# Two attention stages that share buffers, later group ends, and softmax maxima and inverse sums carried to their rows by DMA through DRAM instead of by TensorE transposes

## The reference

```python
def _causal_softmax_attention(q, k, v):
    ...
        z = jnp.einsum('bhqd,bhkd->bhqk', qi, k).astype(jnp.float32) * scale
        causal = key_pos[None, :] <= q_pos[:, None]
        p = jax.nn.softmax(jnp.where(causal, z, neg), axis=-1)
        return jnp.einsum('bhqk,bhkd->bhqd', p.astype(v.dtype), v)
...
    o_mla = o_mla.transpose(0, 2, 1, 3).reshape(B, S, MLA_WIDTH) * jax.nn.silu(g_mla)
    mixed = jnp.concatenate([o_sb, o_mla], axis=-1)
    return x + gate * (mixed @ w_out)
```

## Time and profile before

| | us |
|---|---|
| median of 3 runs | 2162.2 |
| lowest and highest | 2160.57, 2168.74 |
| profiled execution | 2165.11 |
| its span, first to last instruction | 2163.4 |
| TensorE matmuls busy | 1924.4 (89%) |
| VectorE busy | 1239.1 (57%) |
| GpSimd busy | 1011.9 (47%) |
| ScalarE busy | 953.3 (44%) |

### The profile page before, as it was taken

One profiled execution on the slowest core, in us unless ns is written; L12 is line 12 of the kernel. 1 busy time (PEld: TensorE's weight loads), 2 busy tenths in 40 slices (PEclk: granted clock), 3 DMA queues, 4 the chain that ended last, 5 costly groups with the idle time before them and its releaser, 6 DMA issues. The chain is left out here.

```text
span 2163.4 us, 32782 instructions
## 1 busy us (share of the span) xinstructions
PE 1924.4 (89%) x9697; PEld 1571.3 (73%) x9697; DVE 1239.1 (57%) x1862; ACT 953.3 (44%) x1894; POOL 1011.9 (47%) x1035
## 2 busy tenths in 40 slices
PE   6389999997999997598989889499999999985998
PEld 1258888886999996377777777278787887874886
DVE  1731111114555555598989888378787888872111
ACT  1521111114333333377767667367676775762000
POOL 0400000000333333199889889567777776781122
PEclk9689999998999998699999999789899998997999
DMA  8326563445455554732517150453342534105664
GB/s 293 106 78 185 155 180 107 136 151 186 163 195 185 187 179 136 180 72 62 142 36 180 32 125 0 110 115 79 78 107 51 117 78 86 52 20 194 194 183 147
DMA packets 225371, 273.69 MB, mean 127 GB/s; under 512 B 13776, under 2 KB 161520, under 8 KB 219616
## 3 DMA queue, kind: packets, MB, share of 16 engines
q1 hardware_dynamic: 219936, 259.76, 42.4%
q10 hardware_dynamic: 5312, 12.58, 1.8%
HBM read 159.06 MB, written 109.05 MB: 124 GB/s over the span
## 5 line engine op out<-in xcount | busy, mean ns | idle before, releaser
L1944 POOL TENSOR_TENSOR mla_wl<-mla_w,mla_wh 128x512 fp32r<-128x512 f32 (+1 forms) x320 | 374.6, 1184 | 158.5 <-ACT mla_wh L1980 150.6
L1465 POOL TENSOR_TENSOR sb_wl<-sb_wf,sb_wh 128x512 fp32r<-128x512 f32 (+2 forms) x240 | 285.5, 1190 | 19.2
L1563 DVE TENSOR_TENSOR_SCAN sb_w<-sb_kp,sb_w,sb_beside 128x512 f32<-128x512 f32 x192 | 245.4, 1278 | 36.9 <-ACT sb_kp L1486 20.6
L1979 ACT ACTIVATE mla_w<-mla_zt 128x512 f32<-128x512 f32 (+1 forms) x320 | 170.6, 533 | 126.8 <-PE mla_zt L2133 62.9
L568 PE MATMUL pt_po<-h_hi,pt_wh 128*128 128x512 f32 x512 | 200.3, 391 | 9.4 <-DVE pt_wl L499 9.4
L569 PE MATMUL pt_po<-h_lo,pt_wh 128*128 128x512 f32 x512 | 199.9, 390 | 0.0
L570 PE MATMUL pt_po<-h_hi,pt_wl 128*128 128x512 f32 x512 | 199.9, 390 | 0.0
L2021 DVE TENSOR_REDUCE mla_nmx<-mla_zn 128x1 f32<-128x512 f32 (+2 forms) x320 | 191.8, 601 | 11.2 <-PE mla_zn L2100 7.3
L1486 ACT ACTIVATE sb_kp<-sb_z 128x512 f32<-128x512 f32 (+3 forms) x320 | 168.4, 530 | 33.7 <-PE sb_z L1646 16.1
L1643 PE MATMUL sb_z<-sb_kk,sb_qh 128*128 128x512 f32 (+3 forms) x320 | 132.8, 415 | 54.8 <-ACT sb_kp L1486 30.3
L1463 POOL CAST sb_wh<-sb_wf 128x512 fp32r<-128x512 f32 (+2 forms) x240 | 142.1, 592 | 72.3 <-ACT sb_wf L1497 61.8
(11 more groups left out here) (229 smaller groups left out, 4384.5 us busy)
## 6 DMA issues: line engine op xcount, KB each, us to landing
mod_wada<-in_w_ada SPq DMA_DIRECT2D x6, 2048.0 KB, 8.4
qk_mla<-tk_th SPq DMA_DIRECT2D x64, 192.0 KB, 2.1
qk_mla<-tk_tl SPq DMA_DIRECT2D x64, 192.0 KB, 2.3
mod_x<-in_x ACTq DMA_DIRECT2D x16, 512.0 KB, 4.2
pt_w<-in_w_feat SPq DMA_DIRECT2D x16, 512.0 KB, 6.0
hT<-h_hi SPq DMA_DIRECT2D x16, 512.0 KB, 3.6
hT<-h_lo SPq DMA_DIRECT2D x16, 512.0 KB, 5.2
qk_sb<-pt_oh SPq DMA_DIRECT2D x32, 256.0 KB, 2.5
```

The source lines that it names most:

```text
L1465: nc.gpsimd.tensor_tensor(wl[i][:, lo:GW], wf[i][:, lo:GW], wh[i][:, lo:GW].bitcast(F32), ALU.subtract).then_inc(s_plo, 1)
L1563: nc.vector.tensor_tensor_scan(kept, keeps, beside[:, 0:b - a], 1.0 if u["n"] == 0 else w[u["g"]][:, u["r"], b:b + 1], ALU.mult, ALU.bypas ...
L1944: nc.gpsimd.tensor_tensor(wl[i][:, cols], w[i][:, cols], wh[i][:, cols].bitcast(F32), ALU.subtract).then_inc(s_lo, 1)
L1979: nc.scalar.activation(w[i][:, cols], zt[x % 2][:, cols], ACT.Exp).then_inc(s_w, 1)
```

## The change

Three things are changed together.

Buffers: `attend_sb` and `attend_mla` use the same SBUF tensors for k, q and v (`shared`). In the last pair of the first stage SP loads q, k and v of the first softmax head into buffers that are free by then; only `kl` is left for the start of `attend_mla`. The output weights are loaded during the last pair of `attend_mla`, behind the gate. The stick-breaking stage starts when k and the last 512 queries of its first head have landed (`s_first`), part of them issued from ScalarE's queue.

Group ends: in `attend_sb`, `high` and `low` come two turns later. In `attend_mla` the quotient comes at `LAG` + 5 instead of + 2, `high` at + 7 instead of + 2, `low` and the store at + 8 instead of + 3.

Rows: `to_row` and `spread` leave TensorE, `row` and `totals` leave ScalarE. SP stores `nm` as 512 separate elements to `maxima` in DRAM, waits until they have landed, and loads them as one row into `qh`. In the same way it stores `inv` to `inverses`, waits, and loads them spread over 64 partitions into `scale`. SP now goes through the turns as the other engines do, with these steps in the order of `run`. `nm` and `inv` have two buffers each.

```diff
-        buf = {x: [m.sb(f"{x}{i}", [P, S], F32R) for i in range(2)] for x in ("kk", "qh", "ql")}
-        v = [m.sb(f"v{i}", [P, NB, P], F32R) for i in range(2)]
+        buf = {"kk": shared.kh, "qh": shared.qh, "ql": shared.ql}
+        v = shared.v
...
-            for hp in range(2):
-                load_qk(0, hp)
+            late = slice((GROUPS - 1) * GW, S)
+            for at in range(2):
+                sp.dma_start(buf["kk"][0][at * HD:(at + 1) * HD, :].bitcast(F32), qk[at, H * HD:H * HD + HD, :]
+                             ).then_inc(s_first, 16)
+            for dst, l in (("qh", 0), ("ql", 1)):
+                for at in range(2):
+                    sp.dma_start(buf[dst][0][at * HD:(at + 1) * HD, 0:late.start].bitcast(F32), qk[l, 0:HD, 0:late.start]
+                                 ).then_inc(s_qk[0], 16)
+
+            sp.sem_inc(s_qk[0], 32)
             load_v(0, 0)
+            load_qk(0, 1)
...
+                sp.wait_ge(s_z, it * U + U // 2)
+                sp.sem_inc(s_step, 1)
                 if not last:
-                    sp.wait_ge(s_z, it * U + U // 2)
-                    sp.sem_inc(s_step, 1)
                     load_qk(it + 1, 0)
-                    sp.wait_ge(s_pv, it * T + T // 2)
-                    sp.sem_inc(s_step, 1)
+                else:
+
+                    for dst, which, l, sem in ((shared.qh, 0, 0, shared.s_qkh), (shared.kh, 1, 0, shared.s_qkh),
+                                               (shared.ql, 0, 1, shared.s_qkl)):
+                        sp.dma_start(dst[0][0:QK, :].rearrange("p (n c) -> p n c", n=NB).bitcast(F32),
+                                     qkM[which, l, :, :, 0:P].rearrange("n p c -> p n c")).then_inc(sem, 16)
+                sp.wait_ge(s_pv, it * T + T // 2)
+                sp.sem_inc(s_step, 1)
+                if not last:
                     load_v(it + 1, 0)
+                else:
+                    sp.dma_start(v[0][:].bitcast(F32), vM[:, :, 0:P].rearrange("n p c -> p n c")).then_inc(shared.s_v, 16)
...
+            late = slice((GROUPS - 1) * GW, S)
+            for dst, l in (("qh", 0), ("ql", 1)):
+                for at in range(2):
+                    act.dma_start(buf[dst][0][at * HD:(at + 1) * HD, late].bitcast(F32), qk[l, 0:HD, late]
+                                  ).then_inc(s_first, 16)
...
-                for body, after in ((half_sum, AFTER), (high, AFTER + 1)):
+                for body, after in ((half_sum, AFTER), (high, AFTER + 3)):
...
-                for body, after in ((finish, AFTER), (low, AFTER + 2)):
+                for body, after in ((finish, AFTER), (low, AFTER + 4)):
...
-                if n in (0, U // 2):
+                if n == 0 and isinstance(it, int):
+
+                    pe.wait_ge(s_first, 96)
+                elif n in (0, plan.groups[0]["units"] if isinstance(it, int) else 0, U // 2):
                     pe.wait_ge(s_qk[hp], it * 96 + 96)
...
-    delays = dict(nm=-AHEAD, pm=2 - AHEAD, row=2 - AHEAD, sum=LAG, inv=LAG, spread=LAG + 1, half=LAG, sums=LAG + 1, add=LAG,
-                  gate=LAG, quotient=LAG + 2, mh=LAG + 2, ml=LAG + 3)
-    TAIL = LAG + 3
+    delays = dict(nm=-AHEAD, row=-AHEAD, sum=LAG, inv=LAG, spread=LAG, half=LAG, add=LAG,
+                  gate=LAG, quotient=LAG + 5, mh=LAG + 7, ml=LAG + 8, store=LAG + 8)
+    TAIL = LAG + 8
...
-        ps = m.ps("ps", [P, GW])
+        ps = m.ps("ps", [P, QG])
...
+            def to_row(it, hp, n):
+
+                g, head = plan.groups[n]["g"], it * 2 + hp
+                sp.wait_ge(s_nm, groups(n, it, hp) + 1)
                 sp.sem_inc(s_step, 1)
-                load_qk(it, 1)
-                reached(sp, s_pv, turns(0, it, 0))
+                sp.dma_start(maxima[bass.ds(head, 1), n, :].rearrange("o (r p) -> p (o r)", p=P),
+                             nm[n % 2][:].bitcast(F32), allow_slow_non_contiguous=True).then_inc(s_max_out, 16)
+                sp.wait_ge(s_max_out, 16 * groups(n, it, hp) + 16)
                 sp.sem_inc(s_step, 1)
-                load_v(it, 1)
-                if not start:
-                    store(it - 1, G - 1)
-
-                sp.dma_start(gate[:], gates[bass.ds(it, 1), :, :].rearrange("o p n -> p (o n)")).then_inc(s_gate, 16)
-                if not last:
-                    sp.wait_ge(s_zt, turns(0, it, 1))
+                sp.dma_start(qh[hp][QK:KP, g * GW:(g + 1) * GW].bitcast(F32), maxima[bass.ds(head, 1), n, :]
+                             ).then_inc(s_row[n % 2], 16)
+
+            def spread(it, hp, n):
+
+                g, hb, head = plan.groups[n]["g"], hp * HD, it * 2 + hp
+                sp.wait_ge(s_inv, groups(n, it, hp) + 1)
+                sp.sem_inc(s_step, 1)
+                sp.dma_start(inverses[bass.ds(head, 1), n, :].rearrange("o (r p) -> p (o r)", p=P), inv[n % 2][:],
+                             allow_slow_non_contiguous=True).then_inc(s_inv_out, 16)
+                sp.wait_ge(s_inv_out, 16 * groups(n, it, hp) + 16)
+                sp.sem_inc(s_step, 1)
+
+                reached(sp, s_scale, 16 * groups(n, it, hp))
+                sp.sem_inc(s_step, 1)
+
+                reached(sp, s_quot, pair_groups(n, it - 1) + 1)
+                sp.sem_inc(s_step, 1)
+                sp.dma_start(scale[hb:hb + HD, g * GW:(g + 1) * GW],
+                             inverses[bass.ds(head, 1), n, :].broadcast_to([HD, GW])).then_inc(s_scale, 16)
+
+            def loads(it, hp, x):
+                last = isinstance(it, int) and it == PAIRS - 1
+                if x == 0 and not (last and hp == 1):
+                    reached(sp, s_zt, turns(0, it, hp))
                     sp.sem_inc(s_step, 1)
-                    load_qk(it + 1, 0)
-                    sp.wait_ge(s_pv, turns(0, it, 1))
+                    load_qk(it + hp, 1 - hp)
+                if x == LAG + 1 and not (last and hp == 1):
+                    reached(sp, s_pv, turns(0, it, hp))
                     sp.sem_inc(s_step, 1)
-                    load_v(it + 1, 0)
-                for n in range(G - 1):
-                    store(it, n)
-
-            body(0, True, False)
-            with sp.Fori(1, PAIRS - 1) as it:
-                body(it, False, False)
-            body(PAIRS - 1, False, True)
-            store(PAIRS - 1, G - 1)
+                    load_v(it + hp, 1 - hp)
+                if x == TAIL + 1 and hp == 0:
+                    reached(sp, s_gated, pair_groups(0, it))
+                    sp.sem_inc(s_step, 1)
+                    sp.dma_start(gate[:], gates[bass.ds(it, 1), :, :].rearrange("o p n -> p (o n)")).then_inc(s_gate, 16)
+                    if last:
+                        for k in range(KD):
+                            sp.dma_start(wout.w[k][:], t["w_out"][0, k * P:(k + 1) * P, :]).then_inc(wout.s_w, 16)
+
+            sp.dma_start(kl[0][0:QK, :].rearrange("p (n c) -> p n c", n=NB).bitcast(F32),
+                         qkS[1, 1, :, :, 0:P].rearrange("n p c -> p n c")).then_inc(s_qkl[0], 16)
+            run(sp, dict(row=to_row, turn=loads, spread=spread, store=store))
...
-            def row(it, hp, n):
-
-                g = plan.groups[n]["g"]
-                act.wait_ge(s_pm, groups(n, it, hp) + 1)
-                nc.scalar.activation(qh[hp][QK:KP, g * GW:(g + 1) * GW], ps[0:1, :], ACT.Copy).then_inc(s_row, 1)
...
-            def totals(it, hp, n):
-
-                hb, g = hp * HD, plan.groups[n]["g"]
-                act.wait_ge(s_spread, groups(n, it, hp) + 1)
-
-                reached(act, s_quot, pair_groups(n, it - 1) + 1)
-                nc.scalar.activation(scale[hb:hb + HD, g * GW:(g + 1) * GW], ps[hb:hb + HD, :],
-                                     ACT.Copy).then_inc(s_scale, 1)
...
-            run(act, dict(row=row, turn=weights, half=v_low, sums=totals, mh=high))
+            run(act, dict(turn=weights, half=v_low, mh=high))
...
-                reached(dve, s_pm, groups(n, it, hp) - 1)
+                reached(dve, s_max_out, 16 * (groups(n, it, hp) - 1))
...
-                reached(dve, s_spread, groups(n, it, hp))
-                nc.vector.reciprocal(inv[:], ps[:, 0:QG]).then_inc(s_inv, 1)
+                reached(dve, s_inv_out, 16 * (groups(n, it, hp) - 1))
+                nc.vector.reciprocal(inv[n % 2][:], ps[:]).then_inc(s_inv, 1)
...
-                dve.wait_ge(s_scale, groups(n, it, hp) + 1)
+                dve.wait_ge(s_scale, 16 * groups(n, it, hp) + 16)
...
-            def to_row(it, hp, n):
-                pe.wait_ge(s_nm, groups(n, it, hp) + 1)
-
-                reached(pe, s_row, groups(n, it, hp))
-
-                reached(pe, s_scale, groups(n, it, hp) - (1 if n == 1 else 2))
-                for r in range(QG):
-                    tp = nc.tensor.transpose(ps[0:1, r * P:(r + 1) * P], nm[n % 2][:, r:r + 1], ident[:])
-                tp.then_inc(s_pm, 1)
...
                 if tn["first"]:
-                    pe.wait_ge(s_row, groups(tn["n"], it, hp) + 1)
```

(31 more changed lines are left out.)

58 lines of the change are left out of this document (33 added, 25 removed).

## The result

The changed kernel takes 2422.2 us in the median of four runs (2417.3 to 2431.8), against 2161.4 for the kernel before: ratio 1.121, interval 1.116 to 1.125. It is 12% slower, far outside the range of the prediction. The profiled execution took 2431.8 us, with a span of 2430.0.

The account below looks back on a forecast made before the run. It took TensorE to bound the second attention stage, stopped by waits for VectorE in `high`. From 2165.1 us, -109 taken away and +101 of waits behind SP's queue gave 2157, put at 2155 us, range 2105 to 2208.

Parts of the forecast that it names:

- the small transfer: Store of `nm` or sums, 512 elements of 4 bytes, to DRAM: taken to land in 3.2 us.
- the upper bound of 6.4 us: Most the element-wise store should take, from the position load of 2048 elements behind 1 MB.
- six changes and the first rows: Added waits in softmax attention: 40 us after even heads, 48 after odd ones, 6 for seven first rows.
- Rival (2): Element-wise store costs 6.4 us, not 3.2: +62 us, 2216; chance 0.32 together with another slower case.
- The loads ahead: Small transfers behind four 768 KB loads at a head's start wait for them; the loads take 18.4 us.
- A: Softmax attention: 64 sets of four transposes leave TensorE, 0.43 us a set, -28 us.
- B: Softmax attention: `high` and `low` come later after the quotient, so waits at odd heads shrink; -43 us, bounds 30 and 57.
- C: Stick-breaking stage: the same later group ends remove waits in `high`; -24 us, bounds 12 and 30.
- E: Start of softmax attention: q, k and v already loaded, but zero rows and first maxima remain; -1 us.
- D: Start of stick-breaking stage: it waits for 1.5 MB instead of 3 MB; -7 us.
- F: End of softmax attention: a round trip through DRAM replaces transposes and a copy; +4 us.
- G: Output stage: with weights loaded early it starts sooner and runs without stops; -10 us, bounds 7 and 12.

Follow-up runs that it names:

- probe: The kernel before plus a last stage where SP alone issues small transfers and waits; 512 neighbouring single elements 9.3 us, 128 of them 8.3.
- probe2: The kernel before plus a last stage of lone stores to DRAM at several spacings; 128 neighbouring elements 8.3 us, 512 elements 64 bytes apart 2.3.
- k5_loads: The changed kernel with the loads of q, k and v issued from ScalarE's queue instead of SP's; 2399.9 us, 1.110.
- k4_direct: k1_merge with the maxima written straight from SBUF into their row of SBUF by four transfers of 128 elements, without DRAM; 2093.4 us, 0.968.
- k1_merge: The changed kernel with maxima and inverse sums back on TensorE transposes; merged buffers, later group ends and early output weights stay; 2099.8 us, 0.970.
- k6_ends: The kernel before with only the later group ends in both attention stages; 2117.7 us, 0.979.
- k8_late: k2_inv with the quotient ten turns behind the inverse, not five, and high, low and store equally later; 2166.1 us, 1.002.
- k2_inv: k1_merge with only the inverse sums by DMA through DRAM, maxima by transposes; 2245.5 us, 1.038.
- k9_rows: The changed kernel with maxima and inverses moved by SBUF to SBUF transfers, no neighbouring DRAM writes, quotient at `LAG` + 10; 2179.8 us, 1.008.

## Why the prediction was wrong

**The step that failed** is in the part on the small transfer: "I take 3.2, nearer the lower bound, since a quarter of those 2048 elements would take under 1.6 us beyond a fixed 1.7". The store takes 9.1 to 9.3 us alone (probe, probe2) and 10.0 in the median of the changed kernel. The row that I scaled from was a load, which reads single elements. The price is one of writing neighbours, and hardly shrinks with the number down to 128 (8.3 us). So the upper bound of 6.4 us did not hold it either, and my own test ("I am wrong if ... their landing without loads ahead is over 4 us") is met in the first row of SP's timeline.

**What followed from it.** At 3.2 us every round trip outside the changes of head fitted its five turns, so the working looked at six changes and the first rows. At 9 neither of the two places with five turns fits, the first row of a head and the quotient (the later rows have nine turns and more). TensorE stood 9.9 us at the first row of h0, with no load ahead of it, where I counted nothing, and 11 to 18 us at those of h1, h3, h5 and h7, where I counted 0.8. Quotients in the middle of odd heads, which I had not priced, waited 1 to 11 us, and then delayed the next maxima. The stops that I did price came where I put them, larger: TensorE stood 24.0, 14.3 and 24.3 us at the second row of h1, h3 and h5 (11.2 expected) and 17.2, 17.4 and 20.5 us, behind VectorE waiting for the scale, in h2, h4 and h6 (13.8 expected). Rival (2) named the right cause with 12 us for 0.6 us of store. At 9.2 that would give 2154 + 120 = 2274 us. It is still 148 short. It counts six changes of head, seven first rows and the end; in the trace TensorE waits for a row at 19 of 32 groups and VectorE for the scale at 15 of 16 quotients, since the price does not grow evenly once the room of five turns is gone. How the 148 us divide is not shown.

**The loads ahead** were priced about right. I had the inverses behind the four loads land 19.5 us after the first load's issue; it was 24.3 (1489.11 to 1513.37). The DMA engines are full until about 1507, 18 us after that issue, as I had it; the store landed 6 us later, where I counted 1.0. So here too the store was mis-sized and not the loads. With the loads in another queue (k5_loads) 99 of the 268 us of waits went, so most of them need no load ahead. Nor do load and store add up: behind 1 MB the store took 11.3 us, not 16. The Trainium skill, "DMA: Bandwidth & Descriptors", Queues, rings and completion order, was my ground for the wait. The inverses did wait for the loads, which agrees, but the rule gives no sum of two times. The rule on one descriptor per element (same page, Rules for kernel authors), which I had read as a warning without a price, is borne out. The page of the profile counts 48,176 DMA packets under 512 bytes, 34,400 more than the 13,776 before; 64 stores of 512 elements are 32,768.

**The terms taken away.** A and B are read from a stage's first matmul to the start of its last product, C and E from the first matmul of the stick-breaking stage to the first of the softmax attention, D from the first load's issue to the first matmul, F from the last product to the first output matmul, G from there to the end of the span:

| term | predicted | measured | by |
|---|---|---|---|
| A transposes | -28 | about -9 | k4_direct against k1_merge, 4.3 us in the stage for half the sets |
| B group ends, softmax | -43 | -38 | k6_ends, stage 546.7 to 509.1 |
| C group ends, stick-breaking | -24 | -11 | k6_ends, 511.6 to 500.3 |
| D start of stick-breaking | -7 | -2 | after, 16.6 to 14.6 |
| E start of softmax attention | -1 | -8 | k1_merge against k6_ends, 500.3 to 492.5 |
| F end of softmax attention | +4 | +14 | after, 19.3 to 33.4 |
| G output | -10 | -6 | after, 196.9 to 191.1 |

B to E and G sum to -65; k1_merge gained 63. B and C came by the mechanism that I had, with the waits in `high` nearly gone; C lies just under its lower bound of 12. For A I took the time that the engine was held in one place for a gain in the whole, and little of it came out; why is not shown, and 4.3 us is hardly clear of noise, as the intervals of the two kernels overlap. D's mechanism failed: the 1.5 MB did not come ahead of the rest. The late part of `ql`, 128 KB a transfer from ScalarE's queue, landed only after 11.5 us, with SP's other loads under way beside it. In E TensorE had waited 17.9 us for `kh`; it now waits 12.1 us for `maskr` from ScalarE, which is neither of the two things that I had in mind. F is the store's price again, twice in a row at the end.

## What to carry to other kernels

Before a tensor is turned through DRAM, look at which addresses the single writes go to: a store of neighbouring 4-byte elements took four times as long as the same store with the elements 64 bytes apart, and a direct transfer from SBUF into the row of SBUF needs no DRAM at all. A round trip cost nothing here where the schedule had room for it (the middle quotients of k8_late) and a stop where it had not (the same ones in k2_inv), so compare it with that room at every place, not only where queues are full. A queue that waits for a landing holds everything behind it: cheap stores alone did not save k9_rows. And moving transfers to another engine's queue moves the time of their issue there: k5_loads lost most of what it won that way.
